# Paged keys transposed in 32x32 blocks on VectorE, the page loads of the key stage split over two queues by partition half

## What is computed

```python
# cache_k, cache_v: (1, n_phys, 128 rows, 8 heads, 128) in float32; page_table: (8 sequences, 16 pages)
idx, valid = dsa_select(iq, iw, ik_all, q_pos, 256)       # the 256 best keys of each query
logits = einsum('bthd,btkhd->bthk', q, k_sel) * ATT_SCALE + bias
p = softmax(where(valid, logits, -inf))
out = einsum('bthk,btkhd->bthd', p, v_sel)
# around it: norm, input projection, prompt attention, gated MLP branch, output projection, ConvFFN, norm
```

## Time and profile before

| what | value |
|---|---|
| median of 3 runs | 1591.89 us (1589.79 to 1596.37) |
| profiled execution, its span | 1593.2 us |
| PE busy | 1471.7 us, 92% |
| DVE busy | 762.0 us, 48% |
| ACT busy | 511.5 us, 32% |
| POOL busy | 234.5 us, 15% |
| queue of SP (q1) | 243.95 MB, 44.5% of 16 DMA engines |
| whole span | 266.58 MB, mean 167 GB/s |

### The profile page before, as it was taken

The page is one execution under the profiler, slowest core; times in us unless marked ns, Lnnn a source line. Parts: engine busy times, 40 slices in busy tenths (PEclk is TensorE's granted clock), DMA queues, the critical chain, the costliest instruction groups (busy, mean ns, idle before and its releaser), DMA issues.

```text
span 1593.2 us, 32571 instructions
## 1 busy us (share of the span) xinstructions
PE 1471.7 (92%) x13518; PEld 1334.5 (84%) x13518; DVE 762.0 (48%) x1030; ACT 511.5 (32%) x818; POOL 234.5 (15%) x371
## 2 busy tenths in 40 slices
PE   7999998979979989899998998899799999999995
PEld 4867798957867778797777998799699999999995
DVE  5288699496514540025540135543555555552123
ACT  4243223324323341023341122122344455442121
POOL 3423234154210000000000000321000110000000
PEclk8899999989999999999999999899799999999998
DMA  5415223122159979999869976133322233223221
GB/s 173 149 27 159 65 80 113 57 96 73 49 188 369 332 249 342 383 358 329 310 223 402 363 258 240 34 125 104 113 80 80 80 90 95 83 98 102 79 83 60
DMA packets 179278, 266.58 MB, mean 167 GB/s; under 512 B 20522, under 2 KB 136539, under 8 KB 178043
## 3 DMA queue, kind: packets, MB, share of 16 engines
q1 hardware_dynamic: 167947, 243.95, 44.5%
q0 software_dynamic: 5104, 11.11, 2.1%
q10 hardware_dynamic: 6080, 9.44, 1.6%
HBM read 240.28 MB, written 24.18 MB: 166 GB/s over the span
## 4 chain that ended last, share of the span: by engine, by line
PE 77%; DVE 8%; DMA 5%; ACT 3%; SPq 2%; issue 2%; POOL 2%; ACTq 0%; DVEq 0%
PE PS L987 14%; PE PS L989 13%; PE PS L988 13%; PE PS L1197 8%; PE PS L1210 4%; PE PS L1245 3%; PE PS L1319 3%; PE PS L1318 3%; PE PS L1317 3%; DMA R<-in_cache_v 3%; PE PS L1028 2%; PE PS L1029 2%; PE PS L1030 2%; PE PS L1173 1%; PE PS L1120 1%
## 5 line engine op out<-in xcount | busy, mean ns | idle before, releaser
L987 PE MATMUL PS<-xn_hi,WH 128*128 128x288 f32 (+1 forms) x1424 | 430.7, 302 | 16.0 <-DVE xn_lo L1614 13.2
L988 PE MATMUL PS<-xn_lo,WH 128*128 128x288 f32 (+1 forms) x1424 | 424.7, 298 | 0.0
L989 PE MATMUL PS<-xn_hi,WL 128*128 128x288 f32 (+1 forms) x1424 | 424.6, 298 | 0.0
L987 PEld LDWEIGHTS PS<-xn_hi,WH 128*128 128x128 f32 (+1 forms) x1424 | 271.1, 190 | 33.1 <-issue 22.2
L988 PEld LDWEIGHTS PS<-xn_lo,WH 128*128 128x128 f32 (+1 forms) x1424 | 271.9, 191 | 0.0
L989 PEld LDWEIGHTS PS<-xn_hi,WL 128*128 128x128 f32 (+1 forms) x1424 | 271.6, 191 | 0.0
L582 DVE TENSOR_TENSOR WL<-W,WH 128x2048 fp32r<-128x2048 f32 (+2 forms) x69 | 145.7, 2112 | 241.6 <-ACT WH L1358 241.6
L1358 ACT ACTIVATE WH<-W 128x2048 fp32r<-128x2048 f32 (+2 forms) x81 | 145.1, 1791 | 90.2 <-PE PS L1319 74.9
L1197 PE MATMUL PS<-CST,R 128*128 128x128 f32 x1024 | 142.7, 283 | 9.8 <-DMA R<-in_cache_k 9.5
L1793 DVE COPY RB<-PS 128x512 f32<-128x512 f32 x128 | 88.3, 691 | 115.7 <-PE PS L1197 115.7
L1197 PEld LDWEIGHTS PS<-CST,R 128*128 128x128 f32 x1024 | 112.1, 143 | 35.9 <-issue 25.7
(11 more groups left out here) (257 smaller groups left out, 2423.2 us busy)
## 6 DMA issues: line engine op xcount, KB each, us to landing
R<-in_cache_k SPq DMA_DIRECT2D x128, 512.0 KB, 5.3
R<-in_cache_v SPq DMA_DIRECT2D x128, 512.0 KB, 7.0
W<-in_w_in SPq DMA_DIRECT2D x30, 1024.0 KB, 5.4
W<-in_w_up SPq DMA_DIRECT2D x44, 512.0 KB, 4.6
W<-in_w_down SPq DMA_DIRECT2D x16, 704.0 KB, 4.4
x_scratch<-xT SPq DMA_DIRECT2D x2, 2304.0 KB, 9.0
W<-in_w_branch_a SPq DMA_DIRECT2D x4, 1024.0 KB, 7.9
W<-in_w_branch_b SPq DMA_DIRECT2D x4, 1024.0 KB, 6.1
```

The costliest lines, as they stand in the source:

```text
L987: pe.matmul(out, hi[:, k, cols], x.hi_block(n)[:, tokens], start=first, stop=False)
L988: pe.matmul(out, hi[:, k, cols], x.lo_block(n)[:, tokens], start=False, stop=False)
L989: return pe.matmul(out, lo[:, k, cols], x.hi_block(n)[:, tokens], start=False, stop=last)
```

## The change

- A key page is loaded as 32 partitions of 16 KB: partition 32·bb + k holds keys 4k to 4k+3, so that four pages (one for each sequence bb) fill 128 partitions, in one of two buffers `KR`.
- DVE transposes the four pages at once in blocks of 32x32, with two instructions of 2048 elements per partition, each into one of three buffers `KTB`. The PE transposes, their banks and the copies by ACT and DVE are gone.
- PE contracts over 4 sequences times 32 head dimensions, with 4 chunks of 32 dimensions in turn: 32 matmuls for four pages, as many as before. The queries lie in `QB`, which POOL clears and ACT fills with 32 small copies.
- SP issues the pages of bb 0 and 1 (partitions 0 to 63), POOL those of bb 2 and 3 (partitions 64 to 127). Value pages stay with SP and keep their form.
- A `KR` buffer is free when both its transposes are done. The first two sets of four pages go out ahead of everything else at the start; ACT issues the mask's way to DRAM and back.
- Side tiles: 2 at 'start', 5 in each key stage, 2 in each softmax, 7 in the value stages (4 and 3), 1 at the end.
- The logits and the value sums use single banks, one instead of two for each tile.

```diff
@@ side tiles @@
-    two, three = {7: 1, 16: 1}, {4: 1, 10: 1, 16: 1}
-    SIDE_V = [two, two, two, three, two, two, three, {4: 1, 10: 1}]
+    SIDE_K = [2, 5, 8, 11, 14]
+    SIDE_V = [{8: 1}, {8: 1}, {8: 1}, {8: 1}, {8: 1}, {8: 1}, {8: 1}, {}]
-    put_side(('start',), 3)
+    put_side(('start',), 2)
...
+        for kp in SIDE_K:
+            put_side(('K', G, kp), 1)
-        put_side(('softmax', G, 0), 1)
+        put_side(('softmax', G, 0), 2)
@@ buffers @@
+        KR = [blocks(R1[:, 4096 * i:4096 * i + 4096], 4) for i in range(2)]
+        KTB = [a.rearrange("p (n k r) -> p n k r", n=16, r=4) for a in (RB[:, 0:2048], R3[:, 0:2048], R3[:, 2048:4096])]
@@ def page_freed(e, seq) @@
+            G, kind, n = seq // 128, seq // 64 % 2, seq % 64
+            if kind == 0 and n >= 8:
+                e.wait_ge(S_("k_transposed"), 32 * G + 2 * (n // 4 - 1))
+            elif kind == 0:
+                e.wait_ge(S_("v_pages_used"), 64 * G - 4 + 4 * (n // 4))
+            elif n < 8:
+                e.wait_ge(S_("k_transposed"), 32 * G + 30 + 2 * (n // 4))
             else:
+                e.wait_ge(S_("v_pages_used"), 64 * G + n - 7)
@@ def load_page(e, seq), new @@
+            page_freed(e, seq)
+            if kind == 0:
+                bb, kp = n % 4, n // 4
+                v = page_id(e, 4 * G + bb, kp)
+                e.dma_start(KR[kp % 2][32 * bb:32 * bb + 32, :, :],
+                            cache_k[0, bass.ds(v, 1)].rearrange("o (k r) h d -> k (o r) (h d)", r=4))\
+                    .then_inc(key_in[kp % 2][bb], 16)
...
@@ SP @@
+            load_quad(0)
+            load_quad(4)
             side_loads('start')
...
             for G in range(2):
+                for kp in range(NPAGES):
+                    load_quad(128 * G + 4 * kp + 8)
+                    if kp:
+                        side_loads('K', G, kp - 1)
@@ POOL @@
+            pool.memset(QB, 0.0).then_inc(S_("queries_cleared"), 1)
+            load_page(pool, 2)
+            load_page(pool, 3)
...
+            for kp in range(2, NPAGES):
+                load_page(pool, 4 * kp + 2)
+                load_page(pool, 4 * kp + 3)
             drained(pool, 'kl', 0, NPG - 1)
@@ PE, key stage @@
+                for kp in range(NPAGES):
...
+                    for u in range(2):
+                        pe.wait_ge(S_("k_transposed"), 32 * G + 2 * kp + u + 1)
+                        keys = KTB[(2 * kp + u) % 3]
+                        for j in range(4):
+                            for c in range(4):
+                                last = pe.matmul(bank('kl', G, kp)[32 * c:32 * c + 32, P * u:P * u + P],
+                                                 QB[:, G, 4 * u + c, j, :],
+                                                 keys[:, 4 * c + j, :, :].rearrange("p k r -> p (k r)"),
+                                                 start=(j == 0), stop=(j == 3))
...
+                    sides('K', G, kp)
@@ ACT @@
+            for G in range(2):
+                for bb in range(4):
+                    for j in range(4):
+                        t = TP + 32 * G + 8 * bb
+                        last = act.activation(QB[32 * bb:32 * bb + 32, G, :, j, 8 * bb:8 * bb + 8],
+                                              qT[32 * j:32 * j + 32, :, t:t + 8], ACT.Copy)
+            last.then_inc(S_("sample_queries"), 1)
+            act.wait_ge(S_("sample_mask"), 1)
+            act.dma_start(mask_scr, S).then_inc(S_("mask_out"), 16)
             sides('start')
+            act.wait_ge(S_("mask_out"), 16)
+            for j in range(4):
+                act.dma_start(MG[32 * j:32 * j + 32, :], mask_scr[0:32, :]).then_inc(S_("mask_in0"), 16)
@@ DVE, key stage @@
+                def transposed(kp):
+                    for bb in range(4):
+                        dve.wait_ge(key_in[kp % 2][bb], 16 * (8 * G + kp // 2 + 1))
+                    for u in range(2):
+                        n = 2 * kp + u
...
+                        dve.transpose(KTB[n % 3].rearrange("p n k r -> p r n k"), KR[kp % 2][:, :, 512 * u:512 * u + 512]
+                                      .rearrange("p r (n d) -> p r n d", n=16))\
+                            .then_inc(S_("k_transposed"), 1)
+                for kp in range(NPAGES):
+                    transposed(kp)
+                    if kp >= 2:
+                        logits(kp - 2)
...
+                    splits('K', G, kp)
```

More of the change, by code:

```diff
@@ L223, in hybrid_kernel @@
     for G in range(2):
-        for n in range(64):
-            single.add('kp', G, n, 0)
-            single.add('kp', G, n, 1)
         for kp in range(NPG):
-            pair.add('kl', G, kp, at=kp % 2)
-        for i, tile in enumerate(side_at['softmax', G, 0] + side_at['softmax', G, 1]):
-            pair.add(*tile, at=(i + 1) % 2)
+            single.add('kl', G, kp)
+            for tile in side_at.get(('K', G, kp), ()):
+                pair.add(*tile)
+        for tile in side_at['softmax', G, 0] + side_at['softmax', G, 1]:
+            pair.add(*tile)
         for g in range(2):
@@ L234, in hybrid_kernel @@
         for b in range(4):
-            pair.add('o', G, b, at=0)
+            single.add('o', G, b)
             for kp in range(NPG):
                 for tile in side_at.get(('V', G, b, kp), ()):
-                    pair.add(*tile, at=1)
+                    pair.add(*tile)
             single.add('ot', G, b, 0)
             single.add('ot', G, b, 1)
-    pair.add(*side[-1], at=1)
+    for tile in side_at['end',]:
+        pair.add(*tile)
     for c in range(8):
@@ L487, in hybrid_kernel @@
         idx_in = [[S_(f"idx_pages_in{a}_{i}") for i in range(4)] for a in range(2)]
+        key_in = [[S_(f"key_page_in{i}_{bb}") for bb in range(4)] for i in range(2)]
         page_in = [S_(f"page_in{i}") for i in range(8)]
@@ L900, in _ @@
             pool.memset(ST[0:1, 110:111], 0.0).then_inc(S_("ring_free"), 1)
[L901 to L905, removed]
+            load_page(pool, 6)
+            load_page(pool, 7)
             pool.wait_ge(S_("sample_queries"), 1)
@@ L1188, in _ @@
             for G in range(2):
[L1189 to L1200, removed]
-                        pe.wait_ge(S_("sample_queries"), 1)
-                    if n:
-                        kp, bb = (n - 1) // 4, (n - 1) % 4
-                        if bb == 0:
-                            claim(pe, 'kl', G, kp)
-                        for u in range(2):
-                            drained(pe, 'kp', G, n - 1, u)
-                            for j in range(4):
-                                h = 4 * u + j
-                                last = pe.matmul(pbank('kl', G, kp)[32 * j:32 * j + 32, u, 0:P],
-                                                 QZ[:, h, 4 * G + bb, :], KTb[(n - 1) % 2][:, h, :],
-                                                 start=(bb == 0), stop=(bb == 3))
-                        if bb == 3:
@@ L1218, in _ @@
                         h = 4 * u + j
-                        last = pe.matmul(pbank('kl', G, NPG - 1)[32 * j:32 * j + 32, u, 0:P],
+                        last = pe.matmul(bank('kl', G, NPG - 1)[32 * j:32 * j + 32, P * u:P * u + P],
                                          QN[:, h, 32 * G:32 * G + 32], kTn[:, h, :], start=True, stop=True)
@@ L1244, in _ @@
                                 h = 4 * u + j
-                                last = pe.matmul(pbank('o', G, b)[32 * j:32 * j + 32, u, 0:HD],
+                                last = pe.matmul(bank('o', G, b)[32 * j:32 * j + 32, HD * u:HD * u + HD],
                                                  PTs[:, u, kp, 32 * j:32 * j + 32], page[:, HD * h:HD * h + HD],
-                                                 start=(kp == 0), stop=(kp == NPG - 1))
+                                                 start=(kp == 0 and u == 0), stop=(kp == NPG - 1),
+                                                 skip_group_check=True)
                         if kp < NPAGES:
@@ L1798, in _ @@
+                for kp in range(NPAGES):
+                    transposed(kp)
+                    if kp >= 2:
+                        logits(kp - 2)
+                    if kp == 13:
                         drained(dve, 'kl', G, 11)
                         dve.tensor_reduce(EARLY, LS[:, :, 0:12 * P], AX_X, ALU.max)
+                    splits('K', G, kp)
+                logits(14)
                 logits(15)
```

87 lines of the change are left out of this document (44 added, 43 removed).

## The result

The changed kernel takes **1708.5 us** (median of 4 runs, 1707.4 to 1713.1) against 1590.8 (4 runs, 1589.0 to 1596.4) beside it: ratio **1.074**, 95% interval 1.071 to 1.077. It is 7% slower. The forecast was 1546, and the time lies above the whole range, 1532 to 1665.

A forecast was written before the change was run, and what follows sets the result against it. PE was taken to set the key stages' pace, with transfers at 416 GB/s the floor; -17 + 4 - 27 + 3 + 4 - 21 + 8 = -46 us from 1593.2 gave 1547, median 1546 us, range 1532 to 1665.

The forecast's parts named there:

- The rate of two half-width transfers: Key-page loads: two transfers to the two partition halves add up to 410 GB/s, bounds 209 to 418.
- The transpose: Key stages: a DVE transpose of 2048 float32 elements takes 2.3 us, bounds 1.2 to 4.6.
- Rival 1: Key-page loads: the halves don't add up, 209 to 252 GB/s, kernel 1621 to 1672 us; chance 0.20.
- T: Key stages: time per round of four pages, forecast 6.4 us; each us of it costs the kernel 30 us.
- rival 3: Key stages: the strided transpose is slow, 4.6 us each, T 10.5 us, kernel 1669 us; chance 0.12.
- First key stage: PE ends it at 563, 17 us earlier, after a first transpose at 460; the mask's round trip is hidden.
- Softmaxes: Both softmaxes: a second side tile in PE's queue adds 4 us to each.
- Value stages: Transfers at 416 GB/s set the pace: 82 and 80 us, 27 and 21 less than before.
- Second key stage: First transpose comes 5 us into it, waiting for value page 60; the stage takes 110 us, +3.
- Clock: Key stages: PE idling between bursts drops to half clock, adding 4 us to each stage.
- The loop formula: Key stages: two buffers alternate, so four pages need (8.6 to landing + 4.6 transposes)/2 = 6.6 us, taken as 6.4.
- 132 us less PE busy time: Key stages: removing the PE transposes of 128 pages, 1.03 us each, takes 132 us of PE work away.

The follow-up runs named there:

- Contiguous transpose: Changed kernel with DVE writing `KTB` without the step of four words, reordering left to PE's reads and the logit addition: 1695.7 us, ratio 1.064.
- Full width: Changed kernel with each key page loaded over all 128 partitions in 4 KB rows, keys then in wrong places: 1656.3 us, ratio 1.040.
- both cures at full length: Changed kernel with key pages over all 128 partitions and transposes of all 2048 elements without the output step: 1601.4 us, ratio 1.006.
- Both: Changed kernel with key pages over all 128 partitions and each transpose cut from 2048 to 1024 elements: 1589.7 us, ratio 0.998.

## Why the prediction was wrong

**The rate of two half-width transfers**: this is the step that failed first, and the larger one. I took 410 GB/s "since the engines themselves move 418 over the same two halves in one transfer". That one transfer and two at once are the same load was assumed; the queues take turns. Measured: 225 and 211 by stage, inside the bounds 209 to 418, at the end of the nearest rows; the data of four pages, with the tiles' share, take 10.4 us and not 5.7. The rule of the Trainium skill that I set against it, "SBUF — State Buffer", "Can I just issue two DMAs to hit both halves?", gives 222; the runs agree that the halves do not add up: 227 for two queues against 220 for one, 3% where the page has 6%.

**The transpose**: the bounds 1.2 to 4.6 held, my value did not. The step that failed is the output step, which no row showed and for which I added nothing. It measured 3.8 us, and without the step 2.29. The Trainium skill's "SBUF — State Buffer", section "Specifications (TRN2)", says that SBUF wants two hits in each 16-byte line for full bandwidth. A step of four float32 words gives one, and the two durations agree with that rule; a step of two words, which would test it, no run has.

**The rivals, and the end of the range.** Rivals 1 and 3 both came true, but that is not why the time passed both prices (1672 and 1669). Rival 1 was priced with T up to 10.6 and rival 3 with 10.5, and with both true T is 10.75: limits side by side hide each other. Each alone has a run. With the rate alone wrong (`Contiguous transpose`) four pages take 10.13 and 10.31 us in the two stages and the kernel 1695.7; with the transposes alone wrong (`Full width`) 9.15 and 9.12, and 1656.3. By the prediction's own 1546 + 30 x (T - 6.4) these would be some 1661 and 1628, and the changed kernel 1676. The 28 to 35 us above that lie outside T: in the start, the value stages and the start of the second key stage, as below. The range ended at 1665, inside the span of rival 1 alone, and left nothing for errors in these terms.

**Pace and sums.** "Each us of T costs 30 us" held: from `Contiguous transpose` to both cures at full length T falls by 2.9 us and the time by 94 (87 by the rule), from the changed kernel to `Full width` by 1.7 and 52 (50). So (10.75 - 6.4) x 30 = 130 of the 162 us between forecast and result. By stage:

- First key stage: the first transpose was forecast at 460 and came at 460.1. The second set came at 468.7 (2.3 late), the third 19.0 later instead of 6.4, as the mask's reads shared its half-rate transfers (12.6), then 13 rounds of 10.75 (56.6 over the forecast), and an end of 9.1 instead of 7.0. Together 73.6, the 636.6 against 563. That the mask is hidden was wrong here: what was to hide it was a rate that wasn't there.
- Softmaxes: +4 each forecast, +3.7 each measured (the 3.0 and 3.4 in an expectation above were read with coarser ends). Right.
- Value stages: 82 and 80 forecast, 93.6 and 89.9 measured, 21.5 in all. I let the transfers run at 416 GB/s throughout, but for 3 us at start and end. They do not, as these stretches of the first one show (columns as above; a tile runs from 711.5 to 719.9):

```profile
655.00:665.00 10.00, 7.71 (x170) 7.28 (x171) 0.34 (x2) 0.00 (x0) 0.00 (x0) 1.00 0.69 236
...
705.00:715.00 10.00, 8.35 (x90) 6.01 (x83) 0.00 (x0) 0.00 (x0) 0.00 (x0) 0.50 1.03 419
715.00:725.00 10.00, 9.27 (x177) 8.67 (x180) 0.61 (x2) 0.92 (x4) 0.00 (x0) 0.97 0.75 265
...
717.00:719.00 2.00, 2.00 (x17) 2.00 (x16) 0.00 (x0) 0.00 (x0) 0.00 (x0) 1.00 0.82 330
719.00:721.00 2.00, 2.00 (x48) 1.84 (x50) 0.00 (x0) 0.65 (x1) 0.00 (x0) 1.00 0.03 12
721.00:723.00 2.00, 2.00 (x82) 2.00 (x76) 0.00 (x0) 0.00 (x0) 0.00 (x0) 1.00 0.86 200
```

  While PE computes a tile it frees no slot. The rate stays at 418 for most of the tile and falls at its end, once the ring of 8 pages is full. Set against 416 GB/s, the first value stage loses 14 us: 7 in its first and last six microseconds, where I had 3, and some 6 around two of its four tiles, where I had none. I had seen that the earlier trace rows gives 353 and 361 for these stages, and took it for PE's share of the pace alone; with fewer tiles the rate stayed at 353 and 350.
- Second key stage: its first transpose came 12.4 us into it, not 5, and then 15 rounds of 10.86: 185 against 110.
- Clock: PE ran at 0.50 for long stretches (460 to 500), as I had said, but with PE off the path I see hardly any cost of it: DVE's transposes wait 4.5 us for PE in the whole kernel. The 8 us were not needed.

**The loop formula** (half of freed-to-landed plus the transposes) holds, but once its terms are measured it is bookkeeping: with two buffers in turn, the time from a freed buffer to its next transpose and the time of its two transposes add up to two rounds, whatever sets the pace. In the changed kernel (13.9 + 7.5)/2 is 10.7 against 10.75 seen, in `Both` (10.6 + 3.9)/2 is 7.2 against 7.24. What it forecasts hangs on its first term, and that was mis-sized even at full width: 10.6 us to the next transpose, where I had 8.6 to the landing, some 25 us in the whole. So with full-width pages and short transposes the answer would have been about 1590, no change, and not 1546: 1546 + 30 x 0.84 + 21 - 8 = 1584 and 4 us at the start (third set at 476.8 and not 472.8), against 1589.7 measured.

**Right**: where the two doubts lay and which was the weakest; their signatures in the profile (share near 1 with 210 to 250 GB/s); that the reordered start gains, though by 10 us and not 17; that PE would leave the bound. Not right was the sign of 132 us less PE busy time: it fell by 69. The transposes are gone, but PE ran at a lower granted clock. The same 2048 key matmuls took 107.1 us instead of 84.4, and the same 2176 value matmuls 91.9 instead of 72.7.

## What to carry to other kernels

Take a rate from a row with the same shape and the same number of transfers in flight; where a forecast depends on two transfers adding up, put the chance on the single one's rate. Where two terms lie in one loop, judge a cure by both together, since alone each shows only a part (here 52 and 19 of 119 us). Let the range have room for the terms outside the loop, too: they were 28 to 35 us here. Split a change with several parts: the order of the first issues, with the mask on ACT's queue, was a gain of 0.7% by itself, and it was buried under a loss of 7%.

## What the runs showed of the hardware

- Pages of 512 KB to 32 partitions each (16 KB per partition), with the tiles' transfers among them, move at 220 GB/s with one queue, and two queues to the two halves of the partitions bring 227; the same pages to 128 partitions (4 KB per partition) bring 271 to 322 at a lower share, in the same loop.
- The 16 engines serve two queues with such pages mostly in turns, of two to five microseconds here, rather than at once; where both are served in one microsecond they move 0.26 MB in it instead of 0.20.
- A float32 transpose of 2048 elements per partition on DVE takes 2.29 us with contiguous output and 3.81 to 3.85 with a step of 16 bytes; 1024 elements with the step take 2.00. PE's reads in runs of 32 elements (395 ns against 388) and the addition in another order (327 against 314) cost next to nothing.
